# First norm of a decoder step: gain applied as x lands by VectorE and GpSimd, 1/rms brought in by a diagonal operand of TensorE's product, squares of x run ahead

## The reference

```python
def rms_norm(x, g):
    xf = x.astype(jnp.float32)
    y = xf * lax.rsqrt(jnp.mean(xf * xf, axis=-1, keepdims=True) + EPS)
    return (y * g.astype(jnp.float32)).astype(x.dtype)

h = rms_norm(x, g_mix_pre)
a, u, v, q, k, vv, gates = jnp.split(h @ w_in, IN_SPLITS, axis=-1)
```

## Time and profile before

| | us |
|---|---|
| median of 3 runs | 1868.69 |
| lowest and highest | 1867.1, 1868.9 |
| the profiled execution | 1867.63 |
| its span (first to last instruction) | 1865.9 |
| TensorE busy in the span | 1817.3 (97%) |
| VectorE, ScalarE, GpSimd busy | 826.0, 559.3, 276.7 |
| first product of the first unit begins at | 23.47 |
| tile 5's turning begins at | 27.03 |
| first unit ends, small parameter blocks begin at | 40.64 |

### The profile page before, as it was taken

How to read it: one execution, slowest core, us unless ns; L and a number is a source line. 1 busy time by engine, 2 the same in 40 slices (tenths; PEclk the granted TensorE clock), 3 DMA queues, 4 the chain that set the end, 5 groups by cost and what they waited for, 6 DMA issues and landing times.

```text
span 1865.9 us, 28821 instructions
## 1 busy us (share of the span) xinstructions
PE 1817.3 (97%) x11113; PEld 1722.3 (92%) x11113; DVE 826.0 (44%) x1079; ACT 559.3 (30%) x882; POOL 276.7 (15%) x321
## 2 busy tenths in 40 slices
PE   6999999999999999999999999999999999999998
PEld 6878787879699899999999879999999999999997
DVE  5565657575334423232242584442134442344436
ACT  5565757471100100000032452221022220122224
POOL 1121212120133211111110220000000010100002
PEclk9999999999999999999999999999999999999999
DMA  5202020205411111111131031111111111111312
GB/s 166 69 24 68 23 68 23 68 23 175 119 44 47 34 51 51 57 34 41 49 137 57 12 137 45 46 54 47 45 45 45 44 40 52 45 45 51 134 31 97
DMA packets 162283, 113.74 MB, mean 61 GB/s; under 512 B 5389, under 2 KB 152213, under 8 KB 161947
## 3 DMA queue, kind: packets, MB, share of 16 engines
q1 hardware_dynamic: 161035, 108.34, 19.5%
q10 hardware_dynamic: 1200, 4.75, 0.7%
HBM read 95.86 MB, written 13.40 MB: 59 GB/s over the span
## 4 chain that ended last, share of the span: by engine, by line
PE 87%; ACT 5%; DVE 4%; issue 2%; DMA 1%; SPq 0%; ACTq 0%; POOL 0%; DVEq 0%; POOLq 0%
PE ps L1484 67%; PE ps L1494 10%; PE misc L1576 3%; PE misc L1470 1%; ACT zl L736 1%; ACT zl L741 1%; PE ps L1750 1%; PE ps L1560 1%; ACT att L753 1%; PE ps L1561 1%; PE ps L1564 1%; PE ps L1566 1%; DVE hn L1334 1%; PE ps L1470 0%; DMA kv_pg<-in_cache_v 0%
## 5 line engine op out<-in xcount | busy, mean ns | idle before, releaser
L1074 DVE TENSOR_TENSOR w_lo<-stage,w_hi 128x1024 fp32r<-128x1024 f32 x148 | 198.4, 1341 | 579.6 <-POOL w_hi L561 579.2
L1484 PE MATMUL ps<-h_hi,w_lo 128*128 128x344 f32 x1896 | 404.2, 322 | 0.8 <-DVE y_lo L1272 0.8
L1484 PE MATMUL ps<-h_lo,w_hi 128*128 128x344 f32 x1896 | 402.8, 321 | 0.0
L1484 PE MATMUL ps<-h_hi,w_hi 128*128 128x344 f32 x1896 | 400.7, 320 | 0.0
L561 POOL TENSOR_SCALAR w_hi<-stage 128x1024 fp32r<-128x1024 f32 x148 | 158.4, 1070 | 1263.1 <-PE ps L1484 1059.6
L1484 PEld LDWEIGHTS ps<-h_hi,w_lo 128*128 128x128 f32 x1896 | 319.5, 188 | 2.9 <-issue 1.4
L1484 PEld LDWEIGHTS ps<-h_lo,w_hi 128*128 128x128 f32 x1896 | 321.2, 189 | 0.0
L1484 PEld LDWEIGHTS ps<-h_hi,w_hi 128*128 128x128 f32 x1896 | 316.3, 188 | 0.0
L967 ACT ACTIVATE up<-ps 128x1032 f32<-128x1032 f32 x44 | 45.5, 1034 | 354.6 <-PE ps L1484 352.9
L1494 PE MATMUL ps<-h_hi,w_lo 128*128 128x344 f32 x408 | 136.7, 335 | 0.0
L1494 PE MATMUL ps<-h_lo,w_hi 128*128 128x344 f32 x408 | 131.0, 321 | 0.0
(11 more groups left out here) (269 smaller groups left out, 2521.1 us busy)
## 6 DMA issues: line engine op xcount, KB each, us to landing
stage<-in_w_in SPq DMA_DIRECT2D x48, 512.0 KB, 3.8
stage<-in_w_up SPq DMA_DIRECT2D x44, 512.0 KB, 3.8
stage<-in_w_down SPq DMA_DIRECT2D x16, 448.0 KB, 3.4
stage<-in_w_branch SPq DMA_DIRECT2D x24, 256.0 KB, 2.7
x_scratch<-trunk SPq DMA_DIRECT2D x1, 4128.0 KB, 12.6
x_back<-x_scratch SPq DMA_DIRECT2D x1, 4128.0 KB, 13.0
x_tok<-in_x_prompt SPq DMA_DIRECT2D x8, 512.0 KB, 8.3
kv_pg<-in_cache_k SPq DMA_DIRECT2D x16, 256.0 KB, 3.6
```

The costliest lines, as they stand in the source:

```text
L1074: V.tensor_tensor(w_lo[par][:, :, :], stage[par][:, :, :], w_hi[par][:, :, :].bitcast(F32), ALU.subtract).then_inc(w_lo_made, 1)
L1484: last = M(ps[par][:, c, :], w[par][:, k, :], x[:, c * CH:(c + 1) * CH], start=(k == 0 and s == 0), stop=(k == n - 1 and s == 2))
```

## The change

Three things are done differently for each tile n of x.

1. The product with the gain doesn't wait for the norm. As soon as the batch has landed, x times g_pre goes to a tile of its own, `xg_tok`. VectorE does it for tiles 0, 1, 2, 4, 6 and 8 (`scaled`), GpSimd for tiles 3, 5 and 7 (`POOL_TILES`), between its first and second weight split.
2. The factor rs comes in later: VectorE multiplies the identity by rs, one number per row, into one of four 128x128 tiles `diag` (`factors`), and TensorE multiplies the block of xg_tok (stationary) by diag (moving). The result is the turned block with the factor in it. It is an ordinary float32 product (`M`) in place of the transposing mode (`T_`), 8 for each tile as before.
3. ScalarE's squares run ahead of its copies: the squares and roots of tiles 5 to 8 come before the copy of tile 4.

```diff
+            pool.wait_ge(gpre_in, 16)
+            for n in POOL_TILES:
+                pool.wait_ge(x_in[batch_of(n)], 16 * len(IN_BATCHES[batch_of(n)]))
+                nc.gpsimd.tensor_tensor(xg_tok[:, n, :], x_tok[:, n, :], g_pre[:, :], ALU.mult).then_inc(xg_pool, 1)
             split_hi(1, 16, None)
...
+            squares(0)
+            root(0)
+            squares(1)
+            squares(2)
+            root(1)
+            high(0)
+            squares(3)
+            squares(4)
+            root(2)
+            high(1)
+            high(2)
+            squares(5)
+            squares(6)
+            root(3)
+            high(3)
+            squares(7)
+            root(4)
+            squares(8)
+            root(5)
+            for n in range(4, NT + 1):
+                high(n)
...
+            def scaled(n):
+                m = P if n < NT else NS
+                b = batch_of(n)
+                dve.wait_ge(x_in[b], 16 * len(IN_BATCHES[b]))
+                V.tensor_tensor(xg_tok[0:m, n, :], x_tok[0:m, n, :], g_pre[0:m, :], ALU.mult).then_inc(xg_vec, 1)
+
+            def factors(b):
...
+                for n in IN_BATCHES[b]:
+                    if n >= 4:
+                        dve.wait_ge(xt_ps, n - 3)
+                    V.tensor_scalar(diag[n % 4][0:m, 0:m], ident[0:m, 0:m], rs[0:m, n:n + 1], None, ALU.mult
+                                    ).then_inc(diag_made, 1)
...
-                        V.scalar_tensor_tensor(x_tok[0:m, n, :], x_tok[0:m, n, :], rs[0:m, n:n + 1], g_pre[0:m, :],
-                                               ALU.mult, ALU.mult).then_inc(xn_made, 1)
...
-                pe.wait_ge(xn_made, n + 1)
+                if n in POOL_TILES:
+                    pe.wait_ge(xg_pool, POOL_TILES.index(n) + 1)
+                else:
+                    pe.wait_ge(xg_vec, n + 1 - sum(i < n for i in POOL_TILES))
+                pe.wait_ge(diag_made, n + 1)
                 if n >= 2:
                     pe.wait_ge(in_free[n % 2], n // 2)
                 for k in range(KT):
-                    t = T_(in_ps[n % 2][:, k * m:(k + 1) * m], x_tok[0:m, n, k * P:(k + 1) * P])
+                    t = M(in_ps[n % 2][:, k * m:(k + 1) * m], xg_tok[0:m, n, k * P:(k + 1) * P], diag[n % 4][0:m, 0:m],
+                          start=True, stop=True)
```

More of the change, by code:

```diff
@@ L187, in build @@
         conv_rows = sb("conv_rows", [2 * FT, 4, P], F32, s_in)
+        xg_tok = sb("xg_tok", [P, NT + 1, D], F32, s_in)
+        diag = [sb(f"diag{i}", [P, P], F32, s_in) for i in range(4)]
         s_in.close()
@@ L324, in build @@
         (
-            params_in, gpre_in, consts, par_ps, par_sb, ss_made, std_made, rs_made, xn_made, xt_ps,
+            params_in, gpre_in, consts, par_ps, par_sb, ss_made, std_made, rs_made, xg_vec, xg_pool, diag_made, xt_ps,
             h_hi_made, w_hi_made, w_lo_made, unit_done, biasp_made, q_hi_made, kf_made, k_hi_made,
@@ L340, in build @@
             "params_in", "gpre_in", "consts", "par_ps", "par_sb", "ss_made", "std_made", "rs_made",
-            "xn_made", "xt_ps", "h_hi_made", "w_hi_made", "w_lo_made", "unit_done", "biasp_made",
+            "xg_vec", "xg_pool", "diag_made", "xt_ps", "h_hi_made", "w_hi_made", "w_lo_made", "unit_done", "biasp_made",
             "q_hi_made", "kf_made", "k_hi_made", "ktok_ps", "ktok_made", "vtok_ps", "vtok_made",
@@ L363, in build, with batch_of @@
         IN_BATCHES = [range(0, 1)] + [range(n, min(n + 2, NT)) for n in range(1, NT, 2)] + [range(NT, NT + 1)]
+        POOL_TILES = (3, 5, 7)
+        def batch_of(n):
+            return next(b for b, tiles in enumerate(IN_BATCHES) if n in tiles)
         PAR_COLS = NORM_COLS + 4 * 2 * FT
@@ L690, in _, with squares @@
             act.wait_ge(consts, NCONST + 5)
[L691 to L707, removed]
+            def squares(n):
+                m = P if n < NT else NS
+                b = batch_of(n)
+                act.wait_ge(x_in[b], 16 * len(IN_BATCHES[b]))
+                act.wait_ge(ss_made, n + 1)
+                A(sq[0:m, 0:D], x_tok[0:m, n, :], ACT.Square, accum_out=ss[0:m, n:n + 1]).then_inc(ss_made, 1)
@@ new lines, in root, with high @@
+            def root(b):
+                n0_, n1_ = IN_BATCHES[b][0], IN_BATCHES[b][-1] + 1
+                m = P if n0_ < NT else NS
+                act.wait_ge(ss_made, n1_ + 1)
+                A(std[0:m, n0_:n1_], ss[0:m, n0_:n1_], ACT.Sqrt, bias=eps[0:m, :], scale=1.0 / D).then_inc(std_made, 1)
+            def high(n):
+                m = P if n < NT else NS
+                act.wait_ge(xt_ps, n + 1)
+                A(h_hi[:, :, n * P:n * P + m],
+                  in_ps[n % 2][:, 0:KT * m].rearrange("p (k t) -> p k t", k=KT), ACT.Copy).then_inc(h_hi_made, 1)
@@ L1075, in split_lo @@
                                 ALU.subtract).then_inc(w_lo_made, 1)
-            dve.wait_ge(gpre_in, 16)
[L1079 to L1087, removed]
-                        V.scalar_tensor_tensor(x_tok[0:m, n, :], x_tok[0:m, n, :], rs[0:m, n:n + 1], g_pre[0:m, :],
-                                               ALU.mult, ALU.mult).then_inc(xn_made, 1)
[L1090 to L1098, removed]
@@ new lines, in scaled @@
+            def scaled(n):
+                m = P if n < NT else NS
+                b = batch_of(n)
+                dve.wait_ge(x_in[b], 16 * len(IN_BATCHES[b]))
+                V.tensor_tensor(xg_tok[0:m, n, :], x_tok[0:m, n, :], g_pre[0:m, :], ALU.mult).then_inc(xg_vec, 1)
+            def factors(b):
+                n0_, n1_ = IN_BATCHES[b][0], IN_BATCHES[b][-1] + 1
+                m = P if n0_ < NT else NS
+                dve.wait_ge(std_made, b + 1)
+                V.reciprocal(rs[0:m, n0_:n1_], std[0:m, n0_:n1_]).then_inc(rs_made, 1)
+                dve.wait_ge(rs_made, b + 1)
+                for n in IN_BATCHES[b]:
[3 more added lines that the diff above has]
+                                    ).then_inc(diag_made, 1)
@@ new lines, in low @@
+            def low(n):
+                m = P if n < NT else NS
+                dve.wait_ge(h_hi_made, n + 1)
+                V.tensor_tensor(h_lo[:, :, n * P:n * P + m],
+                                in_ps[n % 2][:, 0:KT * m].rearrange("p (k t) -> p k t", k=KT),
+                                h_hi[:, :, n * P:n * P + m].bitcast(F32), ALU.subtract
+                                ).then_inc(in_free[n % 2], 1)
+            dve.wait_ge(gpre_in, 16)
+            dve.wait_ge(consts, NCONST + 5)
@@ L1099, in _ @@
+            scaled(0)
+            factors(0)
+            scaled(1)
+            scaled(2)
+            factors(1)
+            low(0)
+            scaled(4)
+            split_lo(0, 0)
+            factors(2)
+            low(1)
+            scaled(6)
+            low(2)
+            factors(3)
+            scaled(8)
+            low(3)
+            factors(4)
+            factors(5)
+            for n in range(4, NT + 1):
+                low(n)
             split_lo(1, 1)
```

## The result

| | before | changed |
|---|---|---|
| median, us | 1868.2 (6 runs, 1867.1 to 1868.9) | 1877.34 (6 runs, 1876.56 to 1878.06) |
| ratio, with its 95% interval | | 1.0046 [1.0036, 1.0056] |
| the profiled execution, us | 1867.63 | 1876.56 |
| tile 5 begins on TensorE | 27.03 | 32.55 |
| first unit ends (by the chain) | 40.71 | 50.07 |

The kernel became slower, as forecast, but by 9.1 us and not by 5.0: just above the forecast's upper end of 1876.5.

A forecast was written before the change was run, and what follows sets the result against it. VectorE bounds the head from 16.5 on, and TensorE has no gap from tile 5 (27.03); 3.2 for TensorE's products, 1.3 for the later tile 5 and 0.5 for the clock make 5.0 more: forecast 1873.0 us, range 1868.5 to 1876.5.

The forecast's parts named there:

- The rival in which VectorE isn't held: Before tile 5: GpSimd's products let VectorE pass, tile 5 begins 2.4 earlier, 1868.4 to 1869.5 us in all; chance 0.13.
- the one with a cheap product: TensorE's turning: the new product costs no more than the transposing one, so the 3.2 go, 1869.8 us; chance 0.05 in all.
- the one in which the half level behind the blocks goes: TensorE behind the parameter blocks: a shifted head spares the half clock level there, 1.3 less, 1871.7 us; chance 0.09.
- The squares ahead: ScalarE: tile 4's copy comes some 3 us after tile 3's, covered by 0.6 to 1, else up to 1 us more.
- the middle: Start of tile 5 on TensorE: 1.3 later, taken between 0.2 (diagonals not held) and 2.4 (held).
- the 0.5 for the clock: TensorE idle before tile 3: its clock level may fall, costing between 0 and about 1 us; 0.5 taken.
- the held path: VectorE's diagonals wait for GpSimd's products until 21.6, h_lo of tile 1 ends at 23.45, tile 5 begins at 29.4, 2.4 later.
- the 3.2: TensorE from tile 5 to the first unit's end: dearer products of tiles 5 to 8 add 3.2 us, nothing hiding it.
- the 2.64 for tiles 5 to 7: TensorE, tiles 5 to 7: each costs 1.95 in place of 1.07, three times 0.88 more.
- The slow rival: GpSimd's products take 2.39 (1874.5 us), or the half clock level also covers tile 4 and the 8 products (1875.8); chance 0.17.

The follow-up runs named there:

- the reordered run: The kernel before with VectorE's queue in another order and GpSimd's second w_hi also waiting for the turning of tile 7: 1871.49 us, 1.0014.
- the idle products: The kernel before with GpSimd's three products of x and the gain added into a spare tile that nobody reads: 1871.11 us, 1.0013.

## Why the prediction was right in direction and wrong in size

**What held.** The views named the right place. TensorE had no gap behind tile 5 before, so its longer products count in full. VectorE and GpSimd take turns, whole instruction by whole instruction. Of the 9.4 us at the end of the unit 0.4 are not in the time of the profiled executions; the rest went straight to the end. The rival in which VectorE isn't held is refuted by the w_lo of 3.29, the one with a cheap product by the 1.78 against 0.87, the one in which the half level behind the blocks goes by the 0.54. The squares ahead were covered as forecast; only turning with the identity uncovered them.

**The step that failed** is "So the head gives 0.2 to 2.4 later; I take the middle, 1.3", with the 0.5 for the clock behind it: 1.8 for the start of tile 5. With x landing as early as before it is 5.2 (32.21 against 27.03). Against the working:

- The diagonals are held. Of the two paths the later one was right, 2.4: 1.1 more than the middle.
- GpSimd's product was sized at 1.89, from rows 6. That line names one tile behind the arrow (`work<-a_raw`): GpSimd adds a tile to a shifted view of itself there. Rows 8 had one with two names, L647 at 2.39, and the changed kernel's product has two names. With 2.2 to 2.4 at each turn and the w_hi behind them, the h_lo of tile 1 ends at 24.80 where the held path had 23.45: 1.35 more.
- The clock fell, and tile 3 took 3.75, tile 4 2.28. Tile 4 ends at 30.97; the held path, moved by 1.35, gives 29.5. That is 1.5 for the clock where the sum had 0.5.

That makes 1.1 + 1.35 + 1.0, or 3.4 above the 1.8. The parts are worked out along the prediction's own path; for the clock, the run with TensorE kept at work gives at most 1.4.

**The term that was mis-sized** is tile 8 in the 3.2. I doubled 0.59 to 1.18, but its 16 records take 1.88, as much as 128 columns do; the run with the ordinary product in the kernel before shows the same. TensorE's part is 3.8 (17.52 against 13.68) and not 3.2. That the 2.64 for tiles 5 to 7 came near the measured 2.5 is partly luck: the product takes 1.78 and not 1.95, and tiles 6 and 7 took 0.87 before and not tile 5's 1.07.

Together 5.0 + 3.4 + 0.6 is 9.0: the difference between the ends of the unit with x equally early (49.72 against 40.71), and near the 9.1 of the medians. The slow rival had the pieces: GpSimd at 2.39 (1874.5) or the lower clock (1875.8). It added each to the middle of the head, not to its held case, and named them as alternatives; they came together.

The Trainium skill ("SBUF — State Buffer", section SBUF: two separate sides) says that an instruction of GpSimd and one of VectorE that needs the shared pair exclude each other for the whole of it, and counts two-port modes of VectorE among those. The first diagonal's 2.17 beside GpSimd's product, against the second's 0.27 behind it, agrees if a diagonal runs in such a mode, which no run here shows. The prediction weighed this rule and still took the middle.

What stays open: the 2.8 us of the reordered run, the 0.7 us that the idle products cost beyond the head, and why x lands 1.1 later in some executions.

## What to carry to other kernels

Moving elementwise work with two SBUF tensors from VectorE to GpSimd can cost more than it saves where VectorE works on SBUF tensors meanwhile: here three such products cost 2.8 us even with nobody waiting for them, while h_lo, which reads PSUM, was not held. When two engines take turns, take a duration from a row with as many different tiles behind the arrow as the new instruction has. When costs lie on one chain, add their bad cases: here the longer wait ahead of TensorE (7.55 us) lowered its clock as well.

## What the runs showed of the hardware

- GpSimd's float32 product of 128x1024 takes 1.89 us with one tile read twice and 2.34 with two tiles, VectorE idle.
- A diagonal of 128x128 on VectorE takes 0.24 to 0.30 alone, and is held by GpSimd like an instruction with two SBUF tensors: 2.17 beside a product, 1.09 beside a w_hi.
- A turned tile takes 0.87 in the transposing mode and 1.78 as an ordinary float32 product at the full level. With blocks of 8x8 it takes 0.59 and 1.88: the ordinary product gains nothing from few columns here.
- The granted clock fell within a gap of 7.55 us on TensorE and stayed at 0.50 over the first 4.5 us of products behind it; in one execution it also fell behind the small blocks of tile 8, with TensorE busy all the time (mean 0.60 over 42.80 to 46.00).
- The same loads of x were ready about 1.1 us apart in different executions of the same head: the square of tile 3 began at 13.60 and 14.63 in the kernel before, at 14.72 and 13.56 in the changed one.
